# Strassen's seven products for pairs of feed-forward units, in an fp32r decoder trunk on Trainium2

## The reference

```python
def swiglu_ffn(x, w_in, w_out):
    gate, up = jnp.split(x @ w_in, 2, axis=-1)
    return (jax.nn.silu(gate) * up) @ w_out
# x = x + 0.5 * swiglu_ffn(rms_norm(x, g), w_in, w_out); w_in: 1024 x 5632, w_out: 2816 x 1024
```

## Time and profile before

| | |
|---|---|
| device time, median of 3 runs | 887.36 us (887.33 to 887.61) |
| span of the profiled execution, first to last instruction | 886.7 us |
| what lies around the span, from the median (the profiled execution's own time is not listed apart) | 0.7 us |
| TensorE busy | 879.4 us (99%) |
| VectorE busy | 564.5 us (64%) |
| ScalarE busy | 421.7 us (48%) |
| GpSimd busy | 78.3 us (9%) |
| mean granted TensorE clock | 0.999 |
| moved by DMA | 181.74 MB, mean 205 GB/s |

### The profile page before, as it was taken

One profiled execution on the slowest core, in us unless ns is written; L12 is line 12 of the kernel. 1 busy time (PEld: TensorE's weight loads), 2 busy tenths in 40 slices (PEclk: granted clock), 3 DMA queues, 4 the chain that ended last, 5 costly groups with the idle time before them and its releaser, 6 DMA issues.

```text
span 886.7 us, 11328 instructions
## 1 busy us (share of the span) xinstructions
PE 879.4 (99%) x4102; PEld 735.1 (83%) x4102; DVE 564.5 (64%) x598; ACT 421.7 (48%) x471; POOL 78.3 (9%) x70
## 2 busy tenths in 40 slices
PE   9999999999999999999999999999999999999997
PEld 8888888889888888888888888888899888888886
DVE  5875565658966766556577556555687666655643
ACT  7644453538845634345345444343663445434432
POOL 1000000428820000000020000000300000000000
PEclk9999999999999999999999999999999999999999
DMA  8987567555254875776728756746575368675722
GB/s 284 289 260 244 195 199 252 165 178 192 71 189 138 290 237 184 243 241 216 240 84 296 255 187 212 240 168 210 187 286 169 117 196 270 223 235 164 243 67 83
DMA packets 152812, 181.74 MB, mean 205 GB/s; under 512 B 8205, under 2 KB 137257, under 8 KB 152776
## 3 DMA queue, kind: packets, MB, share of 16 engines
q1 hardware_dynamic: 152184, 180.72, 62.3%
q10 hardware_dynamic: 592, 0.53, 0.2%
HBM read 168.11 MB, written 1.05 MB: 191 GB/s over the span
## 4 chain that ended last, share of the span: by engine, by line
PE 99%; DVE 0%; ACT 0%; POOL 0%; issue 0%; POOLq 0%; DVEq 0%
PE acc L1322 11%; PE acc L1324 11%; PE acc L1323 11%; PE ga L1322 11%; PE ga L1324 10%; PE ub L1324 10%; PE ga L1323 10%; PE ub L1323 10%; PE ub L1322 10%; PE tp L1396 1%; PE ga L1592 1%; PE ga L1509 1%; PE tp L1679 0%; PE ub L1626 0%; PE tp L1605 0%; PE tp L1616 0%
## 5 line engine op out<-in xcount | busy, mean ns | idle before, releaser
L915 DVE TENSOR_TENSOR w_lo<-raw,w_hi 128x2048 fp32r<-128x2048 f32 x143 | 324.6, 2293 | 67.7 <-ACT w_hi L604 67.6
L604 ACT ACTIVATE w_hi<-raw 128x2048 fp32r<-128x2048 f32 x151 | 284.6, 1908 | 20.5 <-DMA raw<-in_ffn_w_in_dram 17.2
L1322 PE MATMUL acc<-w_hi,act_hi 128*128 128x512 f32 x416 | 163.1, 392 | 0.0
L1324 PE MATMUL acc<-w_hi,act_lo 128*128 128x512 f32 x416 | 161.8, 389 | 0.0
L1323 PE MATMUL acc<-w_lo,act_hi 128*128 128x512 f32 x416 | 161.7, 389 | 0.0
L1322 PE MATMUL ga<-w_hi,xn_hi 128*128 128x512 f32 x384 | 150.8, 393 | 0.1
L1324 PE MATMUL ga<-w_hi,xn_lo 128*128 128x512 f32 x384 | 149.5, 389 | 0.0
L1322 PE MATMUL ub<-w_hi,xn_hi 128*128 128x512 f32 x384 | 149.5, 389 | 0.0
L1323 PE MATMUL ga<-w_lo,xn_hi 128*128 128x512 f32 x384 | 149.5, 389 | 0.0
L1323 PE MATMUL ub<-w_lo,xn_hi 128*128 128x512 f32 x384 | 149.5, 389 | 0.0
L1324 PE MATMUL ub<-w_hi,xn_lo 128*128 128x512 f32 x384 | 149.5, 389 | 0.0
(11 more groups left out here) (173 smaller groups left out, 677.3 us busy)
## 6 DMA issues: line engine op xcount, KB each, us to landing
raw<-in_ffn_w_in_dram SPq DMA_DIRECT2D x172, 512.0 KB, 5.1
raw<-in_ffn_w_out_dram SPq DMA_DIRECT2D x88, 512.0 KB, 4.0
xs<-xs SPq DMA_DIRECT2D x176, 64.0 KB, 2.1
raw<-in_sgu_w_in_dram SPq DMA_DIRECT2D x16, 512.0 KB, 4.8
raw<-in_ab_w_in_dram SPq DMA_DIRECT2D x12, 512.0 KB, 5.0
raw<-in_ab_w_out_dram SPq DMA_DIRECT2D x8, 512.0 KB, 3.7
raw<-in_sgu_w_out_dram SPq DMA_DIRECT2D x8, 512.0 KB, 4.2
raw<-in_ffn_w_in_dram SPq DMA_DIRECT2D x8, 256.0 KB, 5.5
```

What stands on the lines that cost most here:

```text
L604: act.activation(w_hi[:, n % RING, :], raw[:, n % RAW, :], ACT.Copy).then_inc(hi_split, 1)
L915: dve.tensor_tensor(w_lo[:, n % RING, :], raw[:, n % RAW, :], w_hi[:, n % RING, :].bitcast(F32), ALU.subtract).then_inc(lo_split, 1)
L1322: pe.matmul(dst, s_hi, m_hi, start=start, stop=False)
L1324: return pe.matmul(dst, s_lo, m_hi, start=False, stop=stop)
```

## The change

In each feed-forward stage units 4 and 5, and units 8 and 9, are worked out together. The tokens (two halves of 128) times the inner dimension (two halves of 512) make a 2 x 2 block matrix, and the slabs of two units make another, so eight block products of 12 matmuls were needed. Now there are seven (Winograd's form of Strassen's scheme): three slabs are multiplied as they are (B11, B21, B22) and four are differences (T1 to T4).

- The four slabs of a pair are loaded in four buffers of their own (`quads`: three in `scratch`, one in `gain`). VectorE makes T1 to T4 there in place (`weight_sum`). Each is split into hi and lo like a slab, so that a stage has 39 slabs to split where it had 33.
- Once in a stage VectorE makes four sums of token blocks from `xn_hi` and `xn_lo`, in ten dependent operations on 128 x 512 elements (`side_sums`); ScalarE and VectorE cut these into hi and lo in the sixth place of the ring, which has five places for slabs meanwhile.
- The products gather in the two small banks `tp`. ScalarE copies three intermediate results out, and VectorE adds a bank to each copy (`keep_first`, `keep_in_gates`, `join`); the copies are in `xs` and in the gate buffer `sgh`.
- The outputs (w_out) of units 0 to 3 and 4 to 7 stand among the products of the pairs, and the last three behind unit 10.
- The hardware loops are written out; what the first mixer loads into `scratch`, the fills of its windows on POOL and the loads for the second mixer come after the last sum of the stage before.

Of the 792 matmuls of a stage 24 go. The core of the diff:

```diff
+    SEVEN = (8, 23)
+    UNITS = (0, 1, 2, 3, 5, 4, 6, 7, 9, 8, 10)
+    PLAIN = (0, 1, 2, 3, 6, 7, 10)
+    B11, B21, T1, T2, B22, T3, T4 = 0, 1, 3, 5, 6, 7, 9
+    QUAD_OF = {B11: 0, B21: 1, T1: 0, T2: 0, B22: 3, T3: 2, T4: 1}
+    SUM_OF = {T1: 1, T2: 2, T3: 3, T4: 4}
+    FFN_SLABS, MIX0_SLABS, MIX1_SLABS = 39, 10, 12
+    SUMS_END = SEVEN[1] + T4 + 1
+    OUT_AT = [z + at for z in SEVEN for at in (2, 4, 8, 10)] + [36, 37, 38]
...
+        quads = [scratch[:, j * SLAB:(j + 1) * SLAB] for j in range(QUADS - 1)]
+        quads.append(gain[:, :, :].rearrange("p a d -> p (a d)"))
+        side = [xs[:, t, HALF:D] for t in range(TT)]
+        sums_hi, sums_lo = (w[:, RING - 1, :].rearrange("p (j a t) -> p j a t", j=4, a=4) for w in (w_hi, w_lo))
+        bank_x, bank_z = tp
...
+                    load_unit(b + 4, w_in, 2)
+                    if k:
+                        sp.wait_ge(slab_used, b)
+                        sp.wait_ge(xs_ready, 4 * k)
+                    load_quad(0, w_in, 0, 4)
+                    load_rows(b + 6, w_in, 0, pair(3 * WIDTH, FF))
+                    load_quad(1, w_in, 1, 4)
+                    load_rows(b + 7, w_in, 1, pair(3 * WIDTH, FF))
+                    load_quad(2, w_in, 0, 5)
+                    to_turn(d + 1)
+                    out_of(0, z + 2)
+                    load_quad(3, w_in, 1, 5)
+                    to_turn(d + 2)
+                    out_of(1, z + 4)
...
+                    split_to(b + 6)
+                    side_hi_of(k, 0, 0)
+                    side_hi_of(k, 1, 1)
+                    hidden_hi(k, 0)
+                    split(b + 7)
+                    gates(1, 1, 2)
+                    split(b + 8)
+                    hidden_hi(k, 1)
+                    side_hi_of(k, 2, 0)
+                    side_hi_of(k, 3, 1)
+                    split(b + 9)
+                    gates(2, 2, 4)
+                    split(b + 10)
+                    hidden_hi(k, 2)
+                    split(b + 11)
+                    gates(3, 3, 6)
+                    seven(k, SEVEN[0], 4)
...
+            def side_sums(first):
+                if first:
+                    side_op(0, tokens(xn_hi, 0, 1), tokens(xn_hi, 1, 1), ALU.add)
+                    side_op(0, side_of(0), tokens(xn_lo, 0, 1), ALU.add)
+                    side_op(0, side_of(0), tokens(xn_lo, 1, 1), ALU.add, True)
+                    side_op(1, side_of(0), tokens(xn_hi, 0, 0), ALU.subtract)
+                    side_op(1, side_of(1), tokens(xn_lo, 0, 0), ALU.subtract, True)
+                else:
+                    side_op(0, tokens(xn_hi, 1, 0), side_of(1), ALU.subtract)
+                    side_op(0, side_of(0), tokens(xn_lo, 1, 0), ALU.add, True)
+                    side_op(1, tokens(xn_hi, 0, 0), tokens(xn_hi, 0, 1), ALU.subtract)
+                    side_op(1, side_of(1), tokens(xn_lo, 0, 0), ALU.add)
+                    side_op(1, side_of(1), tokens(xn_lo, 0, 1), ALU.subtract, True)
...
+            def weight_sum(p, what):
+                to, left, right = {T1: (0, 2, 0), T2: (0, 3, 0), T3: (2, 3, 2), T4: (1, 1, 0)}[what]
...
+                dve.tensor_tensor(quads[to], quads[left], quads[right], ALU.subtract).then_inc(sum_ready, 1)
...
+            def join(p, n, to, bank):
+                dve.wait_ge(slab_used, n)
+                dve.tensor_tensor(to, bank, to, ALU.add).then_inc(joined, 1)
+            def seven(k, z, v):
+                n, p, f, g = base[k] + z, len(SEVEN) * (ffn0[k] // STEPS) + SEVEN.index(z), fill0[k], gated0[k]
+                late = k == 0
+                split(n + 4)
+                weight_sum(p, T2)
+                dve.wait_ge(kept, 3 * p + 1)
+                join(p, n + B21 + 1, side[0], bank_z[:, :])
+                weight_sum(p, T3)
+                hidden_lo(k, v - 1)
+                split(n + 5)
+                weight_sum(p, T4)
+                split(n + 6)
+                split(n + 7)
+                split(n + 8)
+                split(n + 9)
+                dve.wait_ge(kept, 3 * p + 3)
+                join(p, n + B22 + 1, sgh[:, :, 0, :], bank_z[:, :].rearrange("p (a n) -> p a n", a=2))
+                split(n + 10)
+                join(p, n + T3 + 1, sgh[:, :, 1, :], bank_x[:, :].rearrange("p (a n) -> p a n", a=2))
+                split(n + 11)
+                for t in range(TT):
+                    dve.wait_ge(joined, 3 * p + 2 + t)
+                    product_rows(t, g + 2 * v, late, sgh[:, 1, t, :])
+                    to_blocks(t, f + v)
+                split(n + 12)
+                hidden_lo(k, v)
+                product_rows(0, g + 2 * v + 2, late, side[0][:, WIDTH:WIDE])
+                to_blocks(0, f + v + 1)
+                split(n + 13)
+                product_rows(1, g + 2 * v + 2, late, bank_x[:, WIDTH:WIDE])
+                to_blocks(1, f + v + 1)
+                split(n + 14)
...
-                    split_to(b + 5)
-                    dve.wait_ge(blocks_ready, TT * (e + 1))
-                    for t in range(TT):
-                        product_rows(t, g + 2, scaled=late)
-                    hidden_lo(0, e)
-                    for t in range(TT):
-                        to_blocks(t, f + 1)
-                    split_to(b + 7)
...
-                    nxt += 3 * (STEPS - 3)
+                    def unit(v):
+                        for t in range(TT):
+                            product_rows(t, g + 2 * v, late)
+                            to_blocks(t, f + v)
+                    p = len(SEVEN) * (e // STEPS)
+                    split_to(b + 6)
+                    side_sums(True)
+                    hidden_lo(k, 0)
+                    side_lo(k, 0, 0)
+                    side_lo(k, 1, 1)
+                    split(b + 7)
+                    unit(1)
+                    split(b + 8)
+                    weight_sum(p, T1)
+                    side_sums(False)
+                    hidden_lo(k, 1)
+                    side_lo(k, 2, 0)
+                    side_lo(k, 3, 1)
+                    split(b + 9)
+                    unit(2)
+                    split(b + 10)
+                    hidden_lo(k, 2)
+                    split(b + 11)
+                    unit(3)
+                    seven(k, SEVEN[0], 4)
+                    split(b + 23)
+                    weight_sum(p + 1, T1)
+                    hidden_lo(k, 5)
+                    split(b + 24)
+                    unit(6)
+                    split(b + 25)
+                    hidden_lo(k, 6)
+                    split(b + 26)
+                    unit(7)
+                    seven(k, SEVEN[1], 8)
+                    hidden_lo(k, 9)
+                    split(b + 38)
+                    nxt = b + 39
+                    unit(10)
...
+            def multiply(n, bank, tok_hi, tok_lo, start):
+                slab_ready(n)
+                for a in range(4):
+                    o = slice(a * WIDE, (a + 1) * WIDE)
+                    mm = three(bank[:, :], tok_hi[:, a, :], tok_lo[:, a, :], w_hi[:, slot_of[n], o],
+                               w_lo[:, slot_of[n], o], start and a == 0, a == 3, not start)
+                mm.then_inc(slab_used, 1)
+            def seven(k, z, v, outs):
+                n, p, stage = base[k] + z, len(SEVEN) * (ffn0[k] // STEPS) + SEVEN.index(z), ffn0[k] // STEPS
+                first, other = slice(0, P), slice(P, 2 * P)
+                if z == SEVEN[0]:
+                    pe.wait_ge(small_free, small[("norm", k, 1, 1)] + 1)
+                else:
+                    pe.wait_ge(ub_free, fill0[k] + v - 2)
+                multiply(n + B11, bank_x, xn_hi[:, 0:4, first], xn_lo[:, 0:4, first], True)
+                multiply(n + B21, bank_z, xn_hi[:, 4:8, first], xn_lo[:, 4:8, first], True)
+                outs(0)
+                pe.wait_ge(joined, 3 * p + 1)
+                pe.wait_ge(side_ready, 4 * stage + 4)
+                multiply(n + T1, bank_z, sums_hi[:, 0], sums_lo[:, 0], True)
+                outs(1)
+                pe.wait_ge(kept, 3 * p + 1)
+                multiply(n + T2, bank_x, sums_hi[:, 1], sums_lo[:, 1], False)
+                pe.wait_ge(kept, 3 * p + 2)
+                multiply(n + B22, bank_z, sums_hi[:, 2], sums_lo[:, 2], False)
+                pe.wait_ge(kept, 3 * p + 3)
+                multiply(n + T3, bank_x, sums_hi[:, 3], sums_lo[:, 3], False)
+                outs(2)
+                pe.wait_ge(joined, 3 * p + 3)
+                multiply(n + T4, bank_x, xn_hi[:, 4:8, other], xn_lo[:, 4:8, other], False)
+                outs(3)
...
                     unit(b + 2, f + 1)
-                    step(0, True)
-                    step(1, False)
-                    with pe.Fori(1, (STEPS - 3) // 2) as i:
-                        step(0, False, i)
-                        step(1, False, i)
+                    unit(b + 4, f + 2)
+                    unit(b + 6, f + 3)
+                    seven(k, SEVEN[0], 4, step_out)
+                    unit(b + 19, f + 4)
```

(3 more changed lines are left out.)

426 lines of the change are left out of this document (271 added, 155 removed).

## The result

The changed kernel took 1021.36 us (median of 4 runs, 1019.23 to 1022.99) where the kernel before took 887.49 beside it (4 runs, 887.33 to 888.22): 1.151 times as long, with a 95% interval of 1.149 to 1.152. The forecast was 938.0, the range 908 to 958: slower, as said, but 134 us slower instead of 51, so more than twice the loss.

What follows compares the result with a forecast made beforehand. The prediction took TensorE's list of matmuls to bound the kernel (879.4 of 886.7 us busy). It summed 50.5 + 17.2 + 4 + 0.9 - 21.8 = +50.8 and, from a median of 887.36, forecast 938.0 us, range 908 to 958.

Steps and rivals of the forecast that it cites:

- Pace and saving: TensorE: 0.2267 us per matmul, 40.8 us per pair; 24 fewer matmuls in each of 4 stages save 21.8 us.
- First waits: TensorE before slab 4, for the bank after unit 1: 18.0, 16.3, 8.1 and 8.1 us, 50.5 in all.
- The time in hand of 4.0 us: VectorE, stage 3: slack before the product that frees unit 1's bank would delay TensorE, idle time included.
- Second waits: TensorE before slab 6, for the bank after unit 2: 4.3 us a stage, 17.2 in four.
- the rule: TensorE left idle falls to half its clock; 12 matmuls at half pace would cost 2.7 us more per wait.
- Between 0 and 2.6 per stage: I take 1: Third waits, TensorE before slab 21 behind the first pair: 1 us a stage, 4 in all.
- The tails: End of a stage, outputs 8 to 10: no term in the sum, 0 us.
- the constants of the mixer ... 0.9: Stage 0: mixer constants behind unit 10's product (2.2 us) and ahead of the last `act_lo` cost 0.9 us.
- The clock falls: Rival, chance 0.13: 4 x 2.7 us on top for half-pace matmuls behind waits, 949 us.
- Pairs fall behind: Rival, chance 0.05: VectorE lags 2.5 us in each of 8 pairs, 958 us.
- VectorE alone: Rival, chance 0.16: copies don't wait behind slabs, ScalarE never late; waits 32.2 + 14.8, less 21.8, 912 us.
- faster: Rival, chance 0.05: VectorE does the token sums in present idle time, so only the saving counts, 865.6 us.

Runs made afterwards that it cites:

- experiment 5: Experiment 4, with SyncE's slab 22 ahead of copy 5, output slabs of units 4 and 5 ahead of copies 6 and 7, constants ahead of copy 9: 991.28 us.
- experiment 6: Experiment 4, with SyncE's turning copy 5 ahead of quads 2, 3, 1 and slab 22, and copy 6 ahead of quads 1 and 3: 979.43 us.
- kernel 9: Kernel 7 with copies 2, 5, 6 ahead of quads, mixer constants ahead of copy 9, units' first products ahead of the hidden tile's lo part: 919.91 us.
- Experiment 4: Changed kernel with SyncE's loads of slabs 36 and 37 ahead of turning copy 9, and slab 38 ahead of copy 10: 979.77 us.
- kernel 7: Changed kernel, same matmuls, lists of SyncE, ScalarE and VectorE rearranged and token sums moved to GpSimd: 954.54 us (1.0752).
- kernel 11: Against the run before it (925.35 us), both gates ahead of the split of slab 8 or 23, last hidden tile ahead of slab 1's split: 904.93 us.
- experiment 1: Kernel before, with five dependent additions of 128 x 512 on VectorE ahead of unit 1's product in each feed-forward stage: 894.93 us (1.0080).

## Why the prediction was wrong, point by point

- **Pace and saving: right.** 0.2267 us stands in all stretches at full clock, and the first pair of stage 2 takes TensorE from 368.65 to 409.46, 40.8 us, as reckoned. No wait inside a pair.
- **VectorE's costs: right one by one.** Differences 2.28 us (2.25 taken), token sums 0.69 (0.69), lo parts of 128 x 2048 unchanged at 2.28. VectorE's busy time rose by 166 us to 730.5, where 183 and 747 were said. Rows of the page:

```profile
L1352 DVE TENSOR_TENSOR scratch<-gain,scratch 128x2048 f32<-128x2048 f32 x16 | 36.5, 2284 | 0.0
L1310 DVE TENSOR_TENSOR xs<-xs,xn_lo 128x512 f32<-128x512 f32 x24 | 16.6, 692 | 0.8
```

- **First waits: the place right, the sum of 50.4 against 50.5 by luck.** By stage they are 16.3, 15.5, 10.2 and 8.5 against 18.0, 16.3, 8.1 and 8.1, so that 2.5 us too much in stages 0 and 2 and 2.5 too little in 3 and 5 cancel. In stage 0 `act_hi` could start at 42.77, where the forecast had the copies land at 44.7. In stages 3 and 5 a piece was missing: `act_hi` waited 2.65 and 0.91 us for its copy, which I had let cost only in stages 0 and 2. The time in hand of 4.0 us leaves out the 0.42 of the product itself (3.55 with it); the sum, which goes step by step, does not use it. VectorE's timeline of stage 3, beside the earlier trace rows:

```profile
547.48 0.69 DVE L1295 TENSOR_TENSOR act_lo<-xs,act_hi 128x512 fp32r<-128x512 f32 x1 [4.03 <-ACT act_hi L832]
...
551.50 0.41 DVE L1281 TENSOR_TENSOR sgh<-ga,sgh 128x256 f32<-128x256 f32 x1
```

- **Second waits: the place right, the size 5.4 against 17.2.** VectorE's lag is there, but TensorE's unit between runs partly at half clock and so comes later by 7.8 us in four stages: 13.2 together. The other 4.0 us are not placed. That a fall of the clock would hide there the forecast had said itself.
- **The clock: the rule was right and its chance wrong.** The Trainium skill (TensorE: Matmul & The Clock Gate, "HAM oscillation") says that an idle array falls to half clock, and this trace agrees, with 128 matmuls at 0.427 us behind waits. It had a chance of 0.13 and was priced at 10.8 us, behind second waits only; it stood behind each of the 16 waits of 3.00 us and more, 25.5 us, and behind no second wait. The forecast named 4 to 18 us of waiting and still took the clock as likely to hold.
- **"Between 0 and 2.6 per stage: I take 1": wrong.** The third waits are 4.2 to 5.2 us, 18.5 in all. The step looked at VectorE and at copies behind the burst, but not at the other side, at ScalarE's list, where slabs 21 and 22, late in the burst, stand ahead of `act_hi` and the gates (experiments 5 and 6); with both sides moved, in kernel 9, the third waits are 1.3 us and less.
- **The tails: the step that failed most, a term put at nothing.** The sum goes from the pairs to "the constants of the mixer ... 0.9" and says that "the moved small loads cost nothing". Behind the second pair it has no term for the three last output slabs. They stand in SyncE's list each behind a turning copy, which the code of the change shows (`to_turn(d + 9)`, `out_of(8, 36)`, `to_turn(d + 10)`, `out_of(9, 37)`), and ScalarE splits them ahead of the tile that feeds the next copy. That ring is 33.4 us of waits and 9.3 of half-clock matmuls. With the constants (issued from 196.04 on behind copy 10, in stage 0; 11.2 us of waiting where 0.9 was said, and 1.2 at half clock) it makes 54 of the 82 us by which the sum was short. The forecast had the very mechanism, one queue with copies and loads in it, and used it only where loads make a copy late. Experiment 4 showed the reverse, loads late behind copies: two lines, 41.6 us. (By its own terms the sum is 938.2, not 938.0.)
- **The rivals.** "The clock falls" happened. "Pairs fall behind", "VectorE alone" and "faster" did not. None had the tail in it. Against "faster" the forecast's reasons hold, as the lists were; with other lists the loss is nearly all undone (1.0051), which the forecast did not ask.

## What to carry to other kernels

Where the order of work is written out as lists, one per engine, put the lists side by side around each moved wait, SyncE's among them, and ask in both directions: what does this entry hold up that doesn't need it? Do that for the end of a stage as carefully as for the middle, since a ring of waits through a copy, a load and a split cost 3 to 7 us a turn here, and no engine's busy share showed it. And a wait of 3 us or more on TensorE is to be counted with the half-clock matmuls that may stand behind it, 1.2 to 2.4 us for each in the changed kernel.

## What the runs showed of the hardware that I had not expected

- Half pace has no sharp edge in the length of the wait. Behind waits of 3 us and more it never failed to come in the changed kernel. In other runs a wait of 2.27 us (experiment 4) was followed by 7 such matmuls and one of 2.43 (kernel 9) by 6, but one of 3.53 (kernel 7), one of 3.55 (kernel 11) and one of 3.65 (experiment 1) by none. No wait shorter than 2.27 us was followed by such a stretch in the runs here.
- A copy of four 64 KB pieces landed 4.4 us after its first issue with little ahead of it (392.68 to 397.05, experiment 6), but behind the burst of quads it took 8.2 (401.11 to 409.31, the changed kernel) to 8.8 (398.45 to 407.26, experiment 5). So small copies do wait for large ones, here by some 4 us.
- VectorE and GpSimd hold each other up. In kernel 7 GpSimd's addition of 128 x 512 took up to 3.3 us beside a busy VectorE and 1.31 us in stage 5; VectorE's took 0.69 in the changed kernel. Lo parts that overlapped such an addition took up to 3.38 us instead of 2.29. Timelines of GpSimd and VectorE, kernel 7:

```profile
317.69 3.27 POOL L661 TENSOR_TENSOR xs<-xn_hi,xs 128x512 f32<-128x512 f32 x1 [10.79 <-DVE w_lo L1367]
321.04 3.19 POOL L661 TENSOR_TENSOR xs<-xs,xn_lo 128x512 f32<-128x512 f32 x1
770.11 1.31 POOL L661 TENSOR_TENSOR xs<-xs,xn_lo 128x512 f32<-128x512 f32 x1
...
317.53 2.29 DVE L1158 TENSOR_TENSOR w_lo<-raw,w_hi 128x2048 fp32r<-128x2048 f32 x1
319.73 3.38 DVE L1158 TENSOR_TENSOR w_lo<-scratch,w_hi 128x2048 fp32r<-128x2048 f32 x1
```

The Trainium skill (SBUF — State Buffer, "Terms") says that the two arbitrate for one port pair and that the loser blocks fully for an instruction. The trace agrees, if a record is read as waiting plus work. The addition of 317.69 ends at 320.96, 1.14 us after the first lo part has ended at 319.82, about its own 1.31. The next lo part ends at 323.11, 2.15 us after that addition, about its own 2.29. The addition of 321.04 ends 1.12 us later, at 324.23. So they take turns; that is my reading of five records, not an experiment.
